# Linear attention's second pair of heads: scores cut into four lots between quarters of the last gate tile

## The reference

```python
att = jnp.einsum('bhtd,bhsd,bhtsd->bhts', qi, ki, dec)           # scores with decay, causal
o = jnp.einsum('bhtd,bhde->bhte', qi * jnp.exp(bi), s) + jnp.einsum('bhts,bhse->bhte', att, vi)
s_new = s * jnp.exp(bl)[..., None] + jnp.einsum('bhsd,bhse->bhde', ki * jnp.exp(bl - bi), vi)
```

## Time and profile before

| | |
|---|---|
| median of 3 runs | 1372.16 us (1369.86 to 1372.84) |
| the profiled execution | 1372.44 us |
| its span, first to last instruction | 1370.6 us |
| TensorE busy | 1312.6 us, 96% of the span, 9443 matmuls |
| VectorE, ScalarE, GpSimd busy | 46%, 30%, 26% |
| mean granted TensorE clock | 0.989 |

### The profile page before, as it was taken

How to read it: one execution, slowest core, us unless ns; L and a number is a source line. 1 busy time by engine, 2 the same in 40 slices (tenths; PEclk the granted TensorE clock), 3 DMA queues, 4 the chain that set the end, 5 groups by cost and what they waited for, 6 DMA issues and landing times.

```text
span 1370.6 us, 23430 instructions
## 1 busy us (share of the span) xinstructions
PE 1312.6 (96%) x9443; PEld 766.5 (56%) x9443; DVE 636.6 (46%) x1350; ACT 416.5 (30%) x901; POOL 354.8 (26%) x437
## 2 busy tenths in 40 slices
PE   5999989999999999999999999998999999998997
PEld 3454654655566677678445645445654645445653
DVE  4365637848234344473465221337736231327735
ACT  4233302254332222201014212236723212236621
POOL 0100001112224443244430000118741010127731
PEclk9999999999999999999999999999999999999999
DMA  9711011011130100031253415100002514100001
GB/s 314 257 62 61 3 63 53 24 62 62 63 125 2 64 2 3 3 123 62 77 196 84 139 31 184 61 30 22 1 16 56 161 38 165 68 14 1 1 1 61
DMA packets 71530, 96.52 MB, mean 70 GB/s; under 512 B 27639, under 2 KB 35247, under 8 KB 71422
## 3 DMA queue, kind: packets, MB, share of 16 engines
q1 hardware_dynamic: 71050, 94.76, 20.7%
q10 hardware_dynamic: 372, 0.27, 0.1%
HBM read 92.89 MB, written 2.13 MB: 69 GB/s over the span
## 4 chain that ended last, share of the span: by engine, by line
PE 87%; DVE 5%; POOL 3%; ACT 2%; issue 2%; DMA 1%; ACTq 0%; DVEq 0%; POOLq 0%
PE PS L147 83%; PE PS L2691 2%; POOL AR L2978 1%; DVE AR L2797 1%; POOL AR L1995 1%; ACT AR L2919 1%; DMA AR<-in_onehot 1%; PE PS L353 0%; DVE AR L2048 0%; POOL AR L2976 0%; DVE AR L2784 0%; PE PS L1383 0%; ACT AR L2929 0%; PE PS L2106 0%; DVE AR L819 0%
## 5 line engine op out<-in xcount | busy, mean ns | idle before, releaser
L147 PE MATMUL PS<-AR 64*64 64x64 f32 (+14 forms) x8806 | 1238.5, 338 | 31.6 <-ACT AR L2929 6.0
L147 PEld LDWEIGHTS PS<-AR 64*64 64x64 f32 (+5 forms) x8806 | 695.6, 155 | 546.1 <-issue 459.9
L2919 ACT ACTIVATE AR<-AR 128x257 f32<-128x257 f32 (+5 forms) x160 | 84.9, 530 | 98.4 <-DVE AR L2797 88.8
L2797 DVE CUSTOM_DVE_ANT_0 AR<-PS,AR 128x257 f32<-128x257 f32 (+5 forms) x160 | 72.3, 452 | 60.7 <-PE PS L147 43.1
L412 POOL TENSOR_TENSOR AR<-AR 128x1 f32<-128x1 f32 (+4 forms) x26 | 21.8, 840 | 282.5 <-DVE AR L407 235.7
L1175 DVE SCALAR_TENSOR_TENSOR AR<-AR 128x441 f32<-128x441 f32 (+2 forms) x96 | 78.6, 819 | 19.6 <-ACT AR L1132 15.9
L1557 DVE TENSOR_TENSOR AR<-PS,AR 128x256 f32<-128x256 f32 x60 | 25.5, 425 | 101.2 <-PE PS L147 98.1
L2978 POOL TENSOR_SCALAR AR<-AR 128x257 f32<-128x257 f32 (+5 forms) x96 | 53.4, 557 | 58.7 <-DVE AR L2803 51.3
L1684 ACT ACTIVATE AR<-PS 128x512 f32<-128x512 f32 x48 | 28.7, 597 | 93.0 <-PE PS L147 90.6
L2691 PE MATMUL PS<-AR 128*128 128x128 f32 x352 | 50.9, 282 | 5.5 <-DVE AR L2784 3.4
L2976 POOL TENSOR_SCALAR AR<-AR 128x128 f32<-128x128 f32 (+3 forms) x64 | 38.9, 608 | 63.5 <-DVE AR L2803 58.7
(11 more groups left out here) (260 smaller groups left out, 881.3 us busy)
## 6 DMA issues: line engine op xcount, KB each, us to landing
AR<-in_w_in SPq DMA_DIRECT2D x16, 2048.0 KB, 8.9
AR<-in_w_mod SPq DMA_DIRECT2D x6, 2048.0 KB, 13.0
AR<-in_w_out SPq DMA_DIRECT2D x4, 2048.0 KB, 12.7
AR<-in_x SPq DMA_DIRECT2D x8, 512.0 KB, 5.6
AR<-in_w_in SPq DMA_DIRECT2D x4, 1024.0 KB, 7.0
AR<-in_w_o SPq DMA_DIRECT2D x2, 2048.0 KB, 8.2
AR<-in_w_in SPq DMA_DIRECT2D x2, 1664.0 KB, 9.7
AR<-in_w_in SPq DMA_DIRECT2D x12, 256.0 KB, 4.8
```

Source lines behind the costliest of these rows:

```text
L147: return t.matmul(o, l, r, start=s, stop=p, skip_group_check=True)
L2797: v.do.tensor_tensor_reduce(PB[j % NJP][e][:, 0:nk], ps["s", l, j, e][:, 0:nk], bias_for(qb, kind, 2 * a + e, nk), 1.0, 3e38, ALU.add, ALU ...
L2919: a_.do.activation(P, P, ACT.Exp, bias=mn[:, j % NJS, e:e + 1], scale=-1.0, accum_out=su[:, j % NJS, e:e + 1]).then_inc(sa, na("p", l, j, e))
```

## The change

On TensorE, `gate_tile` can be issued in parts, and `gla_scores_t` issues one lot, a quarter of a pair's scores (32 of the 128 matmuls), per call. Pair 0's four lots stand one after the other, as before. For pair 1, the last gate tile is cut into quarters of two matmuls, each followed by one lot. The last gate tile moves from bank 6 to bank 0, the second half of pair 1's scores from banks 0, 1 to 2, 3, and pair 1's outputs from banks 2, 3 and 4, 5 to 4, 5 and 0, 1. The mark that frees the gate's weights, for which `load(6)` waits, now stands behind the last lot. On VectorE, `value(4)`, the fifth value tile's copy, moves ahead of the ends of pair 1's keys. No arithmetic is added or removed.

```diff
-        def gate_tile(a):
-            p = ps.take(t, "ag", a, bank=(6, 6, 7, 6)[a])
-            projN(t, p, w, 0, 512, 2 + a, ("ag", a))
+        def gate_tile(a, lo=0, hi=8):
+            p = ps.banks[(6, 6, 7, 0)[a]] if lo else ps.take(t, "ag", a, bank=(6, 6, 7, 0)[a])
+            for t8 in range(lo, hi):
+                x = mm(t.go, p[:, :], hT[:, t8, 128 * a:128 * a + 128], w[:, t8, :], t8 == 0, t8 == 7)
+            if hi == 8:
+                x.then_inc(st, nt("ag", a))
 
         gla_sums_t(t, 0)
         gate_tile(0)
         gla_ends_t(t, 1, (7, 0, 1, 2))
-        gla_scores_t(t, 0)
-        gla_out_t(t, 0)
+        for a in range(4):
+            gla_scores_t(t, 0, a, (6, 0))
+        gla_out_t(t, 0, (2, 4))
         gla_sums_t(t, 1)
-        for a in range(1, 4):
-            gate_tile(a)
+        gate_tile(1)
+        gate_tile(2)
+        for a in range(4):
+            gate_tile(3, 2 * a, 2 * a + 2)
+            gla_scores_t(t, 1, a, (6, 2))
         nt.mark("weights", 3)
-        gla_scores_t(t, 1)
-        gla_out_t(t, 1)
+        gla_out_t(t, 1, (4, 0))
...
         value(2)
         gla_keys_v(v, 0)
         gla_queries_v(v, 1)
+        value(4)
         gla_ends_v(v, 1)
-        value(4)
         gla_states_v(v, 0)
```

More of the change, by code:

```diff
@@ L695, in gla_sums_t, with gla_scores_t, gla_out_t @@
         x.then_inc(st, nt("ds", hp))
-    def gla_scores_t(t, hp):
+    def gla_scores_t(t, hp, a, banks):
         t.wait_ge(sv, nv["q", hp])
         t.wait_ge(sv, nv["k", hp])
[L703 to L716, removed]
+        if a % 2 == 0:
+            ps.take_two(t, "sc", hp, a // 2, bank=banks[a // 2])
+        p = ps.two("sc", hp, a // 2).rearrange("p (h x) -> p h x", h=2)
+        for n in range(2):
+            for j in range(4):
+                for par in range(2):
+                    tk, o = 128 * a + 64 * par, 128 * (a % 2) + 64 * n + 16 * j
+                    for h in range(2):
+                        r = slice(64 * h, 64 * h + 64)
+                        x = mm(t.go, p[64 * par:64 * par + 64, h, o:o + 16], KI[r, n, j, tk:tk + 64],
+                               QP[r, hp, n, tk + 16 * j:tk + 16 * j + 16], True, True)
+        if a % 2:
+            x.then_inc(st, nt("sc", hp, a // 2))
+    def gla_out_t(t, hp, banks):
         for a in range(4):
             t.wait_ge(sv, nv["s", hp])
-            p = ps.take_two(t, "oa", hp, a, bank=(2, 4)[a % 2]).rearrange("p (h x) -> p h x", h=2)
+            p = ps.take_two(t, "oa", hp, a, bank=banks[a % 2]).rearrange("p (h x) -> p h x", h=2)
             for n in range(2):
```

## The result

| | before | changed |
|---|---|---|
| median | 1370.83 us (5 runs) | 1361.15 us (5 runs) |
| lowest to highest | 1369.86 to 1372.84 | 1360.17 to 1365.13 |
| the profiled execution, its span | 1372.44, 1370.6 us | 1360.17, 1358.4 us |
| mean granted clock of the profiled execution | 0.989 | 0.997 |

The ratio is 0.9931 (95% interval 0.9913 to 0.9949): 9.7 us by the medians, where 6.0 were forecast. The direction and the mechanism held; the time lies under the range of 1363.5 to 1369.4.

A forecast was written before the change was run, and what follows sets the result against it. TensorE, busy 96% of the span, was taken to bound the kernel. Gains of 0.78 + 4.07 + 1.8 - 1.0 = 5.6 us plus 0.4 made 6.0, so 1366.2 us against the median 1372.16; own range 1363.5 to 1369.0, with 0.8 on 1363.5 to 1369.4.

The forecast's parts named there:

- The pause is TensorE's program arriving late: Second pair's scores: TensorE outruns its instruction packets; quarters of gate work hide the fetch, so the 4.07 us pause goes.
- Lots and quarters: Last gate tile and second pair's scores interleaved: scores 3.96 us, outputs 6.7, 18.6 us from gate tile 3's start.
- The switch of shape: Between 128-row and 64-row matmuls: six more switches at 0.17 us each, 1.0 us lost.
- 5.6 us from the end of gate tile 2 on: Last gate tile to second pair's outputs: gain 0.78 + 4.07 + 1.8 - 1.0 = 5.6 us.
- The wait of 0.78 us: Ahead of the second pair's scores, for a Silu emptying bank 6: goes, 0.78 us gained.
- bank 0 and the later load: Bank 0 is empty 3 us before gate tile 3 wants it; the weights' load, some 4.5 us later, stays hidden.
- The fifth values: Ahead of the first pair's sums: the earlier copy lets them start 0.4 us sooner, range 0 to 0.5.
- The clock behind other short idles: Range term: granted clock behind TensorE's other short idles, each worth up to 1.8 us either way.
- 1.8 were in my sum: Last 40 scores and second pair's outputs at full clock: 9.15 us becomes 7.3, 1.8 us gained.
- A short pause that stays: Rival, second pair's scores: quarters don't cover the fetch; 3.0 us gained, 1369.2 us; chance 0.12.
- The pause follows the load: Rival: the pause belongs to the load's traffic and moves into the outputs; 1372.0 us, no change; chance 0.05.
- The mix loses the clock: Rival: gate quarters mixed with tiny matmuls run at half clock; 4.9 us slower, 1377.1 us; chance 0.04.

The follow-up runs named there:

- load_later: The kernel before with only the mark that frees the gate's weights moved behind the second pair's scores; median 1366.99 us, ratio 0.9978.
- no_quarters: The changed kernel with the last gate tile whole and the four lots in one run behind it; median 1365.39 us, ratio 0.9960.
- halves: The changed kernel with the last gate tile in two halves, each followed by two lots; median 1363.50 us, ratio 0.9944.
- lots_only: The changed kernel with the fifth value tile's copy back in its old place; median 1363.53 us, ratio 0.9957.
- lots_again: The changed kernel with the fifth value tile's copy back in its old place, run again for more executions; median 1363.48 us, ratio 0.9955.
- value_only: The kernel before with only the fifth value tile's copy moved ahead of the ends of the second pair's keys; median 1369.19 us, ratio 0.9991.
- after_third: The changed kernel, unchanged, run once more beside three others; median 1361.20 us, ratio 0.9935 against the kernel before.
- after_again: The changed kernel, unchanged, run again for more executions; median 1362.88 us, ratio 0.9939 against the kernel before.
- the repeats: The two further runs of the unchanged changed kernel, against the kernel before; ratios 0.9939 and 0.9935.

## Why the prediction was wrong

Point by point:

- *The pause is TensorE's program arriving late.* Right, and shown: it stays at one place in the instruction stream in load_later and no_quarters, shrinks to 0.9 us when the load moves, and goes when gate matmuls stand between two fetch points. The Trainium skill (Runtime: NRT & Kernel Launch, Instruction fetch mechanics) gives TensorE room for 2048 instructions and calls the crossing of a block's edge "mostly hidden"; the runs show 0.8 to 1.4 us not hidden, 388 and 432 instructions (194 and 216 matmuls with their loads) into a run of tiny matmuls.
- *Lots and quarters, 3.96 us of scores, outputs 6.7, from gate tile 3 to the last output 18.6 us.* Measured 18.4, one unbroken stretch. The switch of shape was 0.13 us (0.16 by halves) and not 0.17.
- *5.6 us from the end of gate tile 2 on.* 5.9 between the two profiles, about 6 in time (lots_only, lots_again).
- *The wait of 0.78 us goes, bank 0 and the later load cost nothing.* Right; no idle stands in the 488 matmuls.
- *The fifth values, 0.4 us.* The idle went from 2.05 to 1.61 us, released by ScalarE's sixth value, as worked out. But the move was worth 1.2 us (value_only, by the ratio) to 2.3 us (after_third against lots_again). **This is the named part of the failed term:** I charged the idle and not the half clock behind it. The rows had it: 104 matmuls of sums and gate took 11.32 us from 132.18 on the earlier trace rows, in the changed kernel 9.71. The half clock stood in four of five profiles with the long idle and in none of nine with the short one, so it is worth about 4/5 of 1.6 us, 1.3 us an execution (an estimate from these profiles).
- *"The clock behind other short idles, each worth up to 1.8 either way."* **This is the step that failed, by its size and sign.** I read one profiled execution of before and took its clock outside the long pause as equal on both sides, a spread around nothing; the runs show it one-sided, because the change shortens an idle that was often followed by half clock. Mean clock rose by 0.0048, which is 6.6 us of lost clock over 1370. Some 1.5 us of that fell in the long pause itself, where nothing ran, and 1.8 were in my sum. That leaves up to 3.3 us that I didn't have, of which the sums' half clock explains about 1.3. For the rest no place was found, so its cause stays open.
- *Luck.* Of the 12.2 us between the two profiled executions some 4 are chance: 0.9 ahead of any edit, 1.6 of clock behind the first pair's pause and 1.6 behind the norm, where other executions of the changed kernel had half clock too (after_again at both places). In the times the luck is smaller: the repeats' 8.4 and 8.9 us against 9.5 by the ratio put up to 1 us of the first comparison's gain down to chance, and their medians (1362.88 and 1361.20 us) still lie under the range.
- *The starting point.* I subtracted 6.0 from 1372.16, a median of three. In the comparison before had 1370.83, and 1370.5 over 63 executions. So 1.3 of the 5.0 us of miss (1366.2 against 1361.15) is the base and 3.7 the gain. In the repeats the gain was 8.4 and 8.9 us by the ratios, where the first comparison had 9.5 by the ratio and 9.7 by the medians.
- *The range.* Its own terms at their ends (7.0 + 0.1 + 1.8 and 5.0 - 0.4 - 1.8) give 1363.3 to 1369.4 and not 1363.5 to 1369.0. The measured time lies under both, so this slip doesn't decide.
- *The rivals.* A short pause that stays: no. The pause follows the load: no (load_later). The mix loses the clock: no, 1.00 for 18.4 us.

What stays open: value_only (1.2 us) and lots_only (5.9) add up to 7.1 by the ratios, the two together gave 8.4 to 9.5. My sum with the sums' half clock, 6.0 + 1.3 = 7.3, falls short by as much. With a kernel that came out at 1.0012 of itself this gap of 1 to 2 us can be scatter; whether fewer idles protect each other was not settled.

## What to carry to other kernels

A long run of tiny matmuls can outrun TensorE's own program: count instructions between "issue" gaps, and if the count is a multiple of the packet, put large matmuls between the fetch points and keep big transfers out of them. Price an idle of TensorE with what runs behind it: compare the same instructions at two places of the trace, and if one place is slower, look at its granted clock. And take the time before from more than three executions where a clock that comes and goes makes steps of 1.5 us.

## What the runs showed of the hardware

- TensorE's program comes in packets of 16 KB, 256 instructions. A run of 64x64 matmuls of 16 columns uses one in 2.0 us at 2.4 GHz; if a fetch is asked for at the packet's edge before, as the packets' times fit, it took 2.0 us plus the pause: an estimate of 2.7 to 3.4 us with the DMA engines free (pauses of 0.76 to 1.42 us in 13 places), 6.0 us under a load at 400 GB/s (pauses of 4.00 to 4.08 us in three).
- An idle of 2.0 us ahead of the first sums was followed by 1.2 GHz in four of five profiles, one of 1.6 us at the same place in none of nine. One of 1.9 us behind the norm, in eight of 13. Which execution is hit no run here settles.
- A switch between 128-row and 64-row matmuls cost 0.13 us in the changed kernel's turns and 0.16 us by halves, as the mean of both directions.
